# Key pages turned by VectorE in 32x32 pieces, and their scores taken on two row halves of TensorE

## What is computed

```python
# moba: 6 heads, past in 4 blocks of 256 keys, each query keeps the top 3 by q . mean(k)
gate = einsum('bhqd,bhnd->bhqn', q, kmean)
s = einsum('bhqd,bhqnkd->bhqnk', q, ks) * scale          # masked, softmax, times v
# fox: 5 heads, all past keys
s = einsum('bhqd,bhkd->bhqk', q, k) * scale + c[t] - c[s]  # c: sum of log forget values
p = softmax(s);  o = einsum('bhqk,bhkd->bhqd', p, v)
```

## Time and profile before

| | |
|---|---|
| median of 3 runs | 1700.94 us (1697.45 to 1704.56) |
| span of the profiled execution | 1707.6 us |
| own time of the profiled execution | the page gives none beside the span |
| TensorE busy | 1613.0 us, 94% |
| VectorE busy | 1042.5 us, 61% |
| ScalarE busy | 674.3 us, 39% |
| GpSimd busy | 181.4 us, 11% |
| DMA | 282.34 MB, mean 165 GB/s |
| block loop of layer 0, scores of block 0 to scores of block 31 | 369.1 to 576.0 us |
| block loop of layer 1, the same | 1203.3 to 1412.5 us |

### The profile page before, as it was taken

One profiled execution on the slowest core, in us unless ns is written; L12 is line 12 of the kernel. 1 busy time (PEld: TensorE's weight loads), 2 busy tenths in 40 slices (PEclk: granted clock), 3 DMA queues, 4 the chain that ended last, 5 costly groups with the idle time before them and its releaser, 6 DMA issues. The chain is left out here.

```text
span 1707.6 us, 35370 instructions
## 1 busy us (share of the span) xinstructions
PE 1613.0 (94%) x13333; PEld 1498.8 (88%) x13333; DVE 1042.5 (61%) x1768; ACT 674.3 (39%) x987; POOL 181.4 (11%) x345
## 2 busy tenths in 40 slices
PE   6999999999898699999999999999898878999998
PEld 6999999976676599999999999999566657999997
DVE  6666557766485566665566665566656735666654
ACT  4333333445453553333343333425555444433322
POOL 0000000022454100000000000000235520000000
PEclk9999999999898899999999999999899988999999
DMA  6444446556677444444444444654677863544444
GB/s 200 149 150 152 152 137 146 127 179 221 208 240 235 146 149 150 150 155 138 148 156 151 153 142 141 161 136 125 214 221 228 257 202 94 180 147 147 141 146 138
DMA packets 282235, 282.34 MB, mean 165 GB/s; under 512 B 43022, under 2 KB 271046, under 8 KB 281990
## 3 DMA queue, kind: packets, MB, share of 16 engines
q1 hardware_dynamic: 266338, 234.28, 44.9%
q0 software_dynamic: 14464, 46.48, 8.5%
q10 hardware_dynamic: 1316, 0.03, 0.1%
HBM read 274.34 MB, written 6.40 MB: 164 GB/s over the span
## 5 line engine op out<-in xcount | busy, mean ns | idle before, releaser
L1707 PE MATMUL PS<-xh,whi 128*128 128x320 f32 x1840 | 576.1, 313 | 13.5 <-DVE xl L1021 7.3
L1707 PE MATMUL PS<-xl,whi 128*128 128x320 f32 x1840 | 569.4, 309 | 0.0
L1707 PE MATMUL PS<-xh,wlo 128*128 128x320 f32 x1840 | 569.3, 309 | 0.0
L687 ACT ACTIVATE whi<-raw 128x2048 fp32r<-128x2048 f32 (+1 forms) x181 | 330.9, 1829 | 565.1 <-PE PS L1707 560.2
L1012 DVE TENSOR_TENSOR wlo<-raw,whi 128x2048 fp32r<-128x2048 f32 (+1 forms) x181 | 395.2, 2185 | 237.2 <-ACT whi L687 235.5
L1707 PEld LDWEIGHTS PS<-xh,whi 128*128 128x128 f32 x1840 | 346.3, 188 | 16.7 <-DVE wlo L1012 10.7
L1707 PEld LDWEIGHTS PS<-xh,wlo 128*128 128x128 f32 x1840 | 346.2, 188 | 1.5
L1707 PEld LDWEIGHTS PS<-xl,whi 128*128 128x128 f32 x1840 | 346.1, 188 | 0.0
L1707 PE MATMUL PS<-hh,whi 128*128 128x320 f32 x704 | 217.7, 309 | 0.0
L1707 PE MATMUL PS<-hl,whi 128*128 128x320 f32 x704 | 217.5, 309 | 0.0
L1707 PE MATMUL PS<-hh,wlo 128*128 128x320 f32 x704 | 217.5, 309 | 0.0
(11 more groups left out here) (271 smaller groups left out, 1842.0 us busy)
## 6 DMA issues: line engine op xcount, KB each, us to landing
raw<-in_ffn_w_gate SPq DMA_DIRECT2D x45, 1024.0 KB
raw<-in_ffn_w_up SPq DMA_DIRECT2D x45, 1024.0 KB
raw<-in_ffn_w_down SPq DMA_DIRECT2D x32, 1024.0 KB
key_pages<-in_cache_moba_k SPq DMA_DIRECT2D x128, 192.0 KB, 3.2
raw<-in_w_in SPq DMA_DIRECT2D x46, 512.0 KB
value_pages<-in_cache_moba_v POOLq DMA_DIRECT2D x118, 192.0 KB, 3.6
key_pages<-in_cache_fox_k SPq DMA_DIRECT2D x128, 160.0 KB, 4.1
value_pages<-in_cache_fox_v POOLq DMA_DIRECT2D x118, 160.0 KB, 4.3
```

The costliest lines, as they stand in the source:

```text
L687: act.activation(whi[s][:, 0:nk, 0:w], raw[s][:, 0:nk, 0:w], ACT.Copy).then_inc(hi_done[s], 1)
L1707: last = te.matmul(out, w[wslot][r, kt, cols], x[r, at, :], start=start and n == 0 and m == 0, stop=stop and n == len(ktiles) - 1 and m == 2)
```

## The change

Key pages are no longer turned by TensorE. The DMAs lay a page out in 32 partitions (token mod 32), 4 groups of tokens and the columns of the heads; a page takes two such groups of 32 partitions, one for each half of its columns, and the two pages of a block stand on partitions 0 to 63 and 64 to 127. A page is loaded in four DMAs instead of two. One instruction of VectorE then turns all 32x32 squares of the block (128 partitions x 1536 elements) from `key_pages` to `keys_t`, both in SBUF, at the head of VectorE's step. The scores of a block are 30 matmuls of 128 columns with 64 rows, 15 for each page, on the row halves 0 to 63 and 64 to 127, into PSUM banks 3 and 4. ScalarE copies them to `weight_rows` and sums them in the same instruction (`copy_scores`); maximum and exponentials then read SBUF. TensorE may start the scores of block i + 1 only once those of block i are copied. Around this: `qz` is laid out anew and both half-rows filled (12 small copies on VectorE, 12 on ScalarE, for 4 on VectorE before), the new tokens' scores take 11 matmuls for 6, the sums of past log forget values are copied in 16 pieces for 2 in layer 0, `copy_outputs` has 6 copies for 4, and the table of constants is smaller.

```diff
+ROW_OF = (0, 32, 16, 8, 40, 48, 64, 96, 80, 72, 104)
+SCORE_CALLS = tuple((g, (24 if g < 3 else 16) * c + PAIR_AT[g], j + c) for c in range(2) for g, j in enumerate((0, 2, 6, 8))) + \
+    ((0, SINGLE_AT[0], 4), (1, SINGLE_AT[1], 4), (2, SINGLE_AT[2], 10), (3, SINGLE_AT[3], 10)) + \
+    ((0, SINGLE_AT[0] + 24, 5), (1, SINGLE_AT[1] + 24, 5), (2, SINGLE_AT[2] + 24, 11))
...
-            key_pages = sb("key_pages", [128, 4, 768], F32, r8)
+            key_pages = sb("key_pages", [128, 2, 4, 384], F32, r8)
...
-            keys_t = [sb(f"keys_t{n}", [128, 12, 128], F32, r9) for n in range(2)]
+            keys_t = [sb(f"keys_t{n}", [128, 4, 384], F32, r9) for n in range(2)]
...
                 def key_page(q, pg):
...
-                        block, a_ = divmod(Q * NPG + pg - 4, 2)
-                        sp.wait_ge(keys_turned, 3 * block + 2 + a_)
+                        sp.wait_ge(keys_turned, block - 1)
                     page = sp.value_load(pages[0:1, q * NPG + pg:q * NPG + pg + 1], min_val=0, max_val=NPOOL - 1)
-                    sp.dma_start(key_pages[:, s, 0:AW], kmv[:, ds(page + L * NPOOL, 1), :].rearrange("p a c -> p (a c)")).then_inc(k_in[s], 16)
-                    sp.dma_start(key_pages[:, s, AW:AW + BW], kfv[:, ds(page + L * NPOOL, 1), :].rearrange("p a c -> p (a c)")).then_inc(k_in[s], 16)
+                    for v in range(2):
+                        r, w = slice(64 * u + 32 * v, 64 * u + 32 * v + 32), 192 - 64 * v
+                        sp.dma_start(key_pages[r, s, :, 0:192],
+                                     kmv[:, ds(page + L * NPOOL, 1), :, 192 * v:192 * v + 192].rearrange("c a t f -> c (a t) f")).then_inc(k_in[s], 16)
+                        sp.dma_start(key_pages[r, s, :, 192:192 + w],
+                                     kfv[:, ds(page + L * NPOOL, 1), :, 192 * v:192 * v + w].rearrange("c a t f -> c (a t) f")).then_inc(k_in[s], 16)
...
+                def copy_scores(i):
+
+                    q, n = divmod(i, NBLK)
+                    Q = L * DB + q
+                    act.wait_ge(block_scores_done, L * BLOCKS + i + 1)
+                    if Q:
+                        act.wait_ge(weights_scaled, 5 * (Q - 1) + n + 1)
+                        settle(act)
+                    act.activation(weight_rows[:, 256 * n:256 * n + 256].rearrange("p (u c) -> p u c", u=2), PS[0:ROWS, 3:5, 128 * n:128 * n + 128], ACT.Copy,
+                                   accum_out=block_sums[:, q, n:n + 1]).then_inc(scores_copied, 1)
...
-                copy_keys(0, 0)
-                copy_keys(0, 2)
                 for i in range(BLOCKS):
...
-                    if i + 1 < BLOCKS:
-                        copy_keys(i + 1, 0)
-                        copy_keys(i + 1, 2)
+                    if n:
+                        copy_scores(i)
                     if i >= 1:
                         block_exp(i - 1)
-                    if n == 0 and q >= 1:
-                        block_factors(q - 1)
+                    if n == 0:
+                        if q >= 1:
+                            block_factors(q - 1)
+                        copy_scores(i)
...
+                def turn_keys(i):
+
+                    block = L * BLOCKS + i
+                    dve.wait_ge(k_in[i % 2], 128 * (block // 2 + 1))
+                    dve.wait_ge(past_in, 2 * block + 2)
+                    if block >= 2:
+                        dve.wait_ge(block_scores_done, block - 1)
+                    settle(dve)
+                    dve.transpose(keys_t[i % 2][:, :, :].rearrange("p t f -> p (t f)"), key_pages[:, i % 2, :, :].rearrange("p t f -> p (t f)")).then_inc(keys_turned, 1)
...
-                    dve.wait_ge(block_scores_done, L * BLOCKS + i + 1)
-                    c = PS[0:ROWS, 3 + n % 2, 256 * (n // 2):256 * (n // 2) + 256]
-                    ch.mark(dve.tensor_reduce(gate_sums[:, 0, n:n + 1], c[0:64], AX.X, ALU.add))
-                    dve.tensor_reduce(minus_max[:, q, n:n + 1], c, AX.X, ALU.max, negate=True).then_inc(block_max_ready, 1)
+                    dve.wait_ge(scores_copied, L * BLOCKS + i + 1)
+                    dve.tensor_reduce(minus_max[:, q, n:n + 1], weight_rows[:, 256 * n:256 * n + 256], AX.X, ALU.max, negate=True).then_inc(block_max_ready, 1)
...
                 for i in range(BLOCKS):
                     q, n = divmod(i, NBLK)
+                    if i + 1 < BLOCKS:
+                        turn_keys(i + 1)
                     if i >= 1:
                         block_stats(i - 1)
...
-                    if i + 1 < BLOCKS:
-                        copy_keys(i + 1, 1)
...
                 def block_scores(i):
...
-                    for u in range(3):
-                        te.wait_ge(*was_read(L, "keys", i, u))
-                    if L * BLOCKS + i >= 2:
-                        te.wait_ge(weights_ready, L * BLOCKS + i - 1)
+                    te.wait_ge(keys_turned, L * BLOCKS + i + 1)
+                    if L * BLOCKS + i:
+                        te.wait_ge(scores_copied, L * BLOCKS + i)
                     settle(te)
-                    o = [PS[32 * g:32 * g + w, 3 + n % 2, 256 * (n // 2):256 * (n // 2) + 256] for g, w in enumerate(GROUP_ROWS)]
-                    k = keys_t[i % 2][:, :, :].rearrange("p (a j) c -> p j a c", a=2)
-                    for m in range(2):
-                        for g, w in enumerate(GROUP_ROWS):
-                            last = te.matmul(o[g], qz[:, q, 2 * g + m, 0:w], k[:, GROUP_TILES[g][m], :, :], start=m == 0, stop=m == 1)
+                    k = keys_t[i % 2][:, :, :].rearrange("p t (j c) -> p j t c", c=32)
+                    for x, (g, at, j) in enumerate(SCORE_CALLS):
+                        w = GROUP_ROWS[g]
+                        for u in range(2):
+                            r = slice(64 * u, 64 * u + 64)
+                            last = te.matmul(PS[32 * g:32 * g + w, 3 + u, 128 * n:128 * n + 128], qz[r, q, at:at + w], k[r, j],
+                                             start=x < 4, stop=x >= len(SCORE_CALLS) - 4)
```

More of the change, by code:

```diff
@@ L158, in constants @@
     put("seqof", (k[:, None] // DS == np.arange(DB)[None, :]).astype(np.float32))
-    bsel = np.zeros((128, 2, 32))
-    for e, (g, at) in enumerate(((0, 0), (0, 8), (1, 0), (1, 8), (0, 16))):
-        bsel[64 + e, g, at:at + DS] = 1.0
+    bsel = np.zeros((128, 40))
+    for e, at in ((0, 0), (3, 8), (2, 16), (1, 24), (4, 32)):
+        for half in range(2):
+            bsel[64 * half + 32 + e, at:at + DS] = 1.0
     put("bsel", bsel)
@@ L180, in ring_units @@
     for L in range(DEPTH):
-        order += [(L, "keys", 0, u) for u in range(3)]
         for i in range(BLOCKS):
             q, n = divmod(i, NBLK)
-            if i + 1 < BLOCKS:
-                order += [(L, "keys", i + 1, u) for u in range(3)]
             if q >= 1:
@@ L210, in read_by_act @@
 def read_by_act(name):
-    return name[1] == "squares" or name[1] == "keys" and name[3] != 1 or name[1] == "weights" and name[3] == 0
+    return name[1] == "squares" or name[1] == "weights" and name[3] == 0
 def ring_reads():
@@ L1162, in past_sums @@
                     dve.wait_ge(past_sums_ready, l + 1)
-                    link(dve.tensor_copy(past[:, l * 320:(l + 1) * 320], PS[:, 6 + l, 0:320]))
+                    for u in range(2):
+                        for t in range(4):
+                            ch.mark(dve.tensor_copy(
+                                past_of(l, u)[:, :, :, t, :],
+                                PS[32 * t:32 * t + 32, 6 + l, 0:320].rearrange("p (h b n u) -> p b n u h", h=BH, b=DB, u=2)[:, :, :, u, :]))
+                    ch.catch_up()
                 give(past_sums_copied)
@@ L1714, in norm @@
                 te.wait_ge(sqsum_ready, w + 1)
-                te.matmul(PS[:, 7, 0:NT], cst("ones"), sqsum[:, 0:NT], start=True, stop=True).then_inc(ms_ready, 1)
+                te.matmul(PS[:, 7, 0:NT], cst("ones").to_broadcast([128, 128]), sqsum[:, 0:NT], start=True, stop=True).then_inc(ms_ready, 1)
             def chunk(s, use):
@@ L1974, in values @@
                         te.wait_ge(v_in[pg], (L * DB + loads) * 32)
-                        for g, c in enumerate(GROUP_PAIR):
-                            te.matmul(PS[groups[g], bank, 0:128], weight_cols[:, pg, groups[g]], page[:, c:c + 128], start=pg == 0, stop=False, skip_group_check=True)
+                        for g in range(4):
+                            te.matmul(PS[groups[g], bank, 0:128], weight_cols[:, pg, groups[g]], pair(page, g), start=pg == 0, stop=False, skip_group_check=True)
                         for g, (c, to) in enumerate(GROUP_REST):
@@ L1980, in values @@
                     new_value = lambda c: toks[0:NS, c + (384 if c < AW else 3 * 384 - AW):]
-                    for g, c in enumerate(GROUP_PAIR):
-                        te.matmul(PS[groups[g], bank, 0:128], weight_cols[0:NS, NPG, groups[g]], new_value(c)[:, 0:128], start=False, stop=True, skip_group_check=True)
+                    for g in range(4):
```

(2 more changed lines are left out.)

215 lines of the change are left out of this document (113 added, 102 removed).

## The result

| | before | after |
|---|---|---|
| median of the runs | 1702.75 us (4 runs) | 1742.21 us (4 runs, 1741.36 to 1743.88) |
| span of the profiled execution | 1707.6 us | 1740.5 us |
| TensorE, VectorE, ScalarE busy | 1613.0, 1042.5, 674.3 us | 1588.3, 1095.6, 642.0 us |

The account below looks back on a forecast made before the run. Block loops bounded by TensorE in most stretches, by DMA in steps 0 to 3, VectorE near its limit in short steps. Terms sum to -14.8 us a layer, twice -29.6: 1671 us; range 1648 to 1740, the forecast's own 1655 to 1688.

Parts of the forecast that it names:

- that is just under the 5.7 us that a step outside step 26 would average: SyncE in the block loop: four key DMAs a page take 2.73 us, a block 5.5 us, within the average step.
- the round of 10.4 us: A key buffer's refill in the block loop: 5.5 us to issue, 3.3 to land, 1.64 to turn, for two steps.
- My rival on SyncE: Key DMA issue slower for the new shape; SyncE sets the pace from 0.65 us between DMAs; 1737 us at 0.75; chance 0.09.
- 6% worse: DMA rate on key loads with shorter runs, 295 against 313 GB/s; costs 0.6 us in steps 0 to 3.
- My rival let this decide from f = 1.55 on: Key DMAs to 32 partitions take f times the engine time; 1753 us at f = 2, 1722 at 1.74; chance 0.16.
- -0.93 us for a step: Block steps bound by TensorE: transposes -1.45 us, new scores +1.41, old scores -0.89.
- eight tiles together: New score matmuls on TensorE: 4 column groups x 2 row halves run at once, 0.84 us instead of 1.41.
- forecast -7.4: Steps 4 to 11 of a layer's block loop, bound by TensorE: 8 x -0.93 us.
- VectorE becomes the bound: Rival in the block loop: steps 13 to 18 -1 us, 19 to 25 +9, 4 to 11 -7; 1700 us; chance 0.17.
- my -0.6: Steps 19 to 25 of a layer: three long steps -2.8 us, four short ones +2.2.
- step 26, which I left alone: One long 20.1 us step of value pages and state sums; no key work matters there, so no change.
- the start: Beginning of each layer's block loop: the first turn stands before the first scores, +1.0 us a layer.

Follow-up runs that it names:

- four wide: Changed kernel with four key DMAs a page of the change's sizes and runs, laid to 128 partitions instead of 32: 1714.15 us, ratio 1.0092 to before.
- the old loads: Changed kernel with keys loaded as before the change, two DMAs a page to 128 partitions, same bytes, keys not in place: 1681.25 us, ratio 0.9888.
- wide loads with early numbers: Changed kernel with two key DMAs a page to 128 partitions, both page numbers of a block read before the wait for the turn: 1674.06 us, ratio 0.9872.

## Why the prediction was wrong

- **SyncE, "that is just under the 5.7 us that a step outside step 26 would average"**: this step failed first. The size was right (0.50 us between DMAs, 2.58 a page, 5.2 a block, forecast 5.5), the conclusion not. I compared a throughput with a mean step and costed the round of 10.4 us at nothing. In the round shown above, from the buffer's release at 406.15 to the end of its next turn at 421.83, it took 15.7 us: 5.8 to issue, 3.65 to land and 1.8 to turn, each near its forecast, and ahead of them 4.5 us in which SyncE was still at the other buffer's DMAs and at two stores, a term that my round didn't have. Adding 1.1 us a page to SyncE alone costs 36 us. My rival on SyncE had the right place and the wrong condition: it was to decide from 0.65 us between DMAs, and it decided at 0.50.
- **DMA, "6% worse" on the keys**: 25% more engine time for each MB. Short runs alone give 10% (four wide: 42.3% for 25.45 MB) and 32 partitions alone 27%; in the changed kernel the two don't add up. My rival let this decide from f = 1.55 on; at 1.27 it cost 39 us. It had priced only the share in stretches near 0.95; the landing time of every round, 1.7 us longer for 192 KB, wasn't in it, though how much of the 39 us that makes isn't shown.
- **TensorE, -0.93 us for a step**: right in direction, the gain under-sized.

```profile
411.87 1.12 PE L1988 MATMUL PS<-keys_t,qz 64*32 64x128 f32 x60
```

  In this block, at 0.27 us a record, the 60 records end after 1.12 us, so starts lie about (1.12 - 0.27) / 60 = 14 ns apart, not 23.6: nearly the case of eight tiles together. With the old loads steps 4 to 11 take 44.4 us (-9.4, forecast -7.4).
- **VectorE**: the turn takes 1.775 us for 1.64. Where keys are in time, the times of the rival "VectorE becomes the bound" show. The kernel with the old loads in steps 4 to 11, 13 to 18, 19 to 25 and 26:

```profile
390.70:435.10 44.40, 40.69 (x859) 28.75 (x858) 37.40 (x103) 23.72 (x88) 16.05 (x40) 0.98 0.79 250
...
441.70:480.80 39.10, 33.39 (x770) 27.78 (x773) 30.39 (x60) 15.36 (x48) 21.12 (x36) 0.79 0.69 223
480.80:526.20 45.40, 33.79 (x719) 28.68 (x718) 37.76 (x83) 17.04 (x55) 29.43 (x58) 0.74 0.83 263
526.20:536.10 9.90, 8.73 (x311) 7.76 (x309) 4.09 (x5) 1.29 (x6) 4.51 (x10) 1.00 0.82 272
```

  Steps 13 to 18 take 39.1 us with VectorE at 78%, where that rival had 39 and I had 34.9. Steps 19 to 25 take 45.4 us with VectorE at 83%, +8.8, near the 46 of that rival and far from my -0.6. That VectorE is what holds them isn't shown: TensorE's clock is 0.79 and 0.74 there as well. And step 26, which I left alone, falls from 20.1 to 9.9 us, so that steps 19 to 26 together come to -1.4; it seems that waiting of step 26 was only moved ahead of it.
- **The sum**: the old loads in the new kernel give 1681.25 us, 21 us under the kernel before (1701.81 in the same series), where I forecast 29.6. The direction of the compute part holds, its size is about 70%, and its parts are off both ways. That wide loads with early numbers come to 1674.06 us, beside a forecast of 1671, is luck in part: some 7 us of it are the early numbers', which I hadn't forecast. By the profiled executions the two loops are 19.3 and 17.2 us shorter, and outside them the kernel is 8.4 us longer; I had looked for nothing there but the start, and what it is stays open. What was missing above all is what the loads take, 61 us.
- **Clock**: I didn't forecast its fall. With time added on SyncE alone it falls too (0.98 to 0.82 in steps 4 to 11), so it follows the waits. But it is 0.79 over the loop of layer 0 even with the old loads, and was 0.92 before, so part of the gain may go there too; what the clock costs isn't shown.

Not settled: how much of the narrow part lies in landing and how much in the slowed value pages; how much of the loss is paid through the clock; and a kernel with wide loads and this turn that has each key in its place, which wasn't tried, since a page on 128 partitions leaves the turn with each token's channels on 32 partitions, and the scores read 64.

## What to carry to other kernels

Where a buffer is refilled behind its last reader, add up the whole round (issue of every DMA in the queue, what else stands in that queue, landing, the reader) and compare it with the shortest steps in a row, not with the mean. When work moves off TensorE into another layout, price the number and the width of the transfers that it asks for: here some 21 us of gain in compute were outweighed by 61 us in loads of the same bytes. And a read that depends on nothing belongs ahead of the wait, not behind it.

## What was not expected of the hardware

- A queue whose key DMAs go to 32 partitions needs 1.27 times the engine time for a MB as with 128 partitions for the same sizes and runs (1.92 and 1.51 points), and the value DMAs beside them, to 128 partitions, the same 1.27.
- A turn of 128 x 1536 float32 elements in 32x32 squares takes 1.775 us on VectorE, 1.16 ns an element of a partition.
- Matmuls of 64 rows, 32 columns and 128 moving float32 columns start some 14 ns apart where a record lasts 0.27 us (60 in 1.12 us), spread over four column groups and two row halves.
